# Second mixer of a two-block transformer: the heads' sums of squares from a rounded square and its rest

## The reference, cut to what matters

```
def rmsnorm(x, g):
    x32 = x.astype(jnp.float32)
    y = x32 * lax.rsqrt(jnp.mean(x32 * x32, axis=-1, keepdims=True) + EPS)
    return (y * g.astype(jnp.float32)).astype(x.dtype)
...
    _, o = lax.scan(step, state0, (qc, kc, vc, bc))
    o = o.transpose(1, 0, 3, 2, 4).reshape(bsz, seq, HGRN_HEADS, HGRN_HEAD_DIM)
...
    o = rmsnorm(o, g_norm_w) * jax.nn.silu(g)
    return jnp.einsum('bsd,de->bse', o.reshape(bsz, seq, D_MODEL).astype(h.dtype), w_out)
```

## Time and profile before

| what | us |
| --- | --- |
| median of 3 runs (2376.27 to 2377.44) | 2377.02 |
| the profiled execution's own time | 2377.56 |
| its span in the trace | 2375.8 |
| TensorE busy | 2364.9 |
| VectorE busy | 1326.7 |
| ScalarE busy | 1031.4 |
| GpSimd busy | 62.4 |

### The profile page before, as it was taken

How to read it: one execution, slowest core, us unless ns; L and a number is a source line. 1 busy time by engine, 2 the same in 40 slices (tenths; PEclk the granted TensorE clock), 3 DMA queues, 4 the chain that set the end, 5 groups by cost and what they waited for, 6 DMA issues and landing times.

```text
span 2375.8 us, 30572 instructions
## 1 busy us (share of the span) xinstructions
PE 2364.9 (100%) x11344; PEld 1946.5 (82%) x11344; DVE 1326.7 (56%) x1950; ACT 1031.4 (43%) x1655; POOL 62.4 (3%) x100
## 2 busy tenths in 40 slices
PE   9999999999999999999999999999999999999999
PEld 7777888888888888888888778888888878888887
DVE  6765744432637867444325776777533556677731
ACT  5555522222447855222324664444322545444420
POOL 1000000000002310000000000000001000000000
PEclk9999999999999999999999999999999999999999
DMA  4112222332221113323322113232323222222332
GB/s 159 54 63 80 89 89 90 105 122 91 81 98 63 54 54 98 97 88 101 116 94 89 63 45 116 89 103 92 107 97 107 80 71 96 92 96 95 104 98 83
DMA packets 69332, 214.30 MB, mean 90 GB/s; under 512 B 7280, under 2 KB 18544, under 8 KB 69232
## 3 DMA queue, kind: packets, MB, share of 16 engines
q1 hardware_dynamic: 67696, 210.72, 26.8%
q0 software_dynamic: 1536, 2.21, 0.3%
HBM read 210.80 MB, written 2.10 MB: 90 GB/s over the span
## 4 chain that ended last, share of the span: by engine, by line
PE 95%; DVE 3%; ACT 2%; issue 0%; DMA 0%; SPq 0%; DVEq 0%; ACTq 0%
PE bank L264 26%; PE bank L266 26%; PE bank L265 26%; PE bank L387 5%; PE bank L379 4%; PE bank L1134 1%; PE bank L1521 1%; PE bank L1125 1%; PE bank L1171 1%; PE bank L2061 0%; DVE w_lo L238 0%; DMA raw<-in_w_fox_v 0%; PE bank L2509 0%; PE bank L2497 0%; DVE h L612 0%
## 5 line engine op out<-in xcount | busy, mean ns | idle before, releaser
L264 PE MATMUL bank<-x_hi,w_hi 128*128 128x512 f32 x1792 | 706.9, 394 | 0.1
L266 PE MATMUL bank<-x_hi,w_lo 128*128 128x512 f32 x1792 | 698.5, 390 | 0.0
L265 PE MATMUL bank<-x_lo,w_hi 128*128 128x512 f32 x1792 | 698.3, 390 | 0.0
L238 DVE TENSOR_TENSOR w_lo<-raw,w_hi 128x1024 fp32r<-128x1024 f32 (+1 forms) x367 | 470.4, 1291 | 239.8 <-ACT w_hi L233 239.0
L233 ACT ACTIVATE w_hi<-raw 128x1024 fp32r<-128x1024 f32 (+1 forms) x367 | 403.7, 1109 | 170.7 <-PE bank L266 102.7
L264 PEld LDWEIGHTS bank<-x_hi,w_hi 128*128 128x128 f32 x1792 | 336.7, 188 | 74.1 <-issue 4.2
L266 PEld LDWEIGHTS bank<-x_hi,w_lo 128*128 128x128 f32 x1792 | 336.8, 188 | 70.9
L265 PEld LDWEIGHTS bank<-x_lo,w_hi 128*128 128x128 f32 x1792 | 336.8, 188 | 70.3 <-issue 1.9
L920 DVE TENSOR_TENSOR bank<-bank,rstd 128x512 f32<-128x512 f32 x176 | 122.6, 699 | 292.9 <-PE bank L266 291.8
L264 PE MATMUL bank<-up_a_hi,w_hi 128*128 128x512 f32 (+1 forms) x748 | 282.0, 377 | 0.0
L266 PE MATMUL bank<-up_a_hi,w_lo 128*128 128x512 f32 (+1 forms) x748 | 281.6, 377 | 0.0
(11 more groups left out here) (361 smaller groups left out, 2714.8 us busy)
## 6 DMA issues: line engine op xcount, KB each, us to landing
raw<-in_w_up SPq DMA_DIRECT2D x176, 512.0 KB, 3.3
raw<-in_w_down SPq DMA_DIRECT2D x64, 704.0 KB, 4.4
raw<-in_w_fox_qk SPq DMA_DIRECT2D x16, 512.0 KB, 3.3
raw<-in_w_hgrn_qf SPq DMA_DIRECT2D x16, 512.0 KB, 3.3
raw<-in_w_fox_out SPq DMA_DIRECT2D x8, 512.0 KB, 3.2
raw<-in_w_hgrn_v SPq DMA_DIRECT2D x8, 512.0 KB, 3.4
raw<-in_w_hgrn_g SPq DMA_DIRECT2D x8, 512.0 KB, 3.2
raw<-in_w_hgrn_out SPq DMA_DIRECT2D x8, 512.0 KB, 3.3
```

The lines of the kernel that those rows point to most:

```text
L238: nc.vector.tensor_tensor(w_lo[:, slot, 0:size], raw[:, slot % 2, 0:size], w_hi[:, slot, 0:size].bitcast(F32), ALU.subtract).then_inc(sem( ...
L264: nc.tensor.matmul(out, w[0], x[0], start=first, stop=False)
L265: nc.tensor.matmul(out, w[0], x[1], start=False, stop=False)
L266: return nc.tensor.matmul(out, w[1], x[0], start=False, stop=last)
```

## The change

The sum of squares is made of two parts, in fp32r. ScalarE squares the output twice: once in full into ho, as before, and once rounded into o_hi. GpSimd subtracts o_hi from ho into o_lo. TensorE multiplies a rounded copy of the ones (ones_r, made once by VectorE) by o_hi and then by o_lo, into the same bank. On TensorE the first product waits for the squares, the second for GpSimd's rest (semaphore hg_split). GpSimd makes the rest of head m - 2 between level 2 and level 3 of head m, and those of the last two heads after its loop.

```diff
+        o_hi = hg.take("o_hi", [P, T], F32R)
+        o_lo = hg.take("o_lo", [P, T], F32R)
+        ones_r = hg.take("ones_r", [P, P], F32R)
...
             def norm(o):
 
+                wait(pe, "hg_kdh", o + 1)
+                wait(pe, "hg_ones", 1)
                 wait(pe, "hg_sq", o + 1)
-                wait(pe, "hg_kdh", o + 1)
-                nc.tensor.matmul(ps[4][:], ones[:], ho, start=True, stop=True).then_inc(sem("hg_ms"), 1)
+                nc.tensor.matmul(ps[4][:], ones_r[:], o_hi[:], start=True, stop=False)
+                wait(pe, "hg_split", o + 1)
+                nc.tensor.matmul(ps[4][:], ones_r[:], o_lo[:], start=False, stop=True).then_inc(sem("hg_ms"), 1)
...
-                        nc.scalar.activation(ho, ps[7][:], ACT.Square).then_inc(sem("hg_sq"), 1)
+                        nc.scalar.activation(ho, ps[7][:], ACT.Square)
+                        nc.scalar.activation(o_hi[:], ps[7][:], ACT.Square).then_inc(sem("hg_sq"), 1)
...
             dve_enter(dve, 2)
+            nc.vector.tensor_copy(ones_r[:], ones[:]).then_inc(sem("hg_ones"), 1)
...
+            def split_squares(o):
+                wait(pool, "hg_sq", o + 1)
+                nc.gpsimd.tensor_tensor(o_lo[:], ho, o_hi[:].bitcast(F32), ALU.subtract).then_inc(sem("hg_split"), 1)
             for m in range(HEADS):
                 wait(pool, "hg_b", m + 1)
                 for l in range(1, LEVELS):
+                    if l == LEVELS - 1 and m >= 2:
+                        split_squares(m - 2)
                     wait(pool, "hg_lv", 5 * (m - 1) + l + 1)
...
+            for o in (HEADS - 2, HEADS - 1):
+                split_squares(o)
```

## The result

The changed kernel takes 2387.97 us (median of 6 runs, 2386.95 to 2388.98), the kernel before 2377.71 us in the same comparison. The ratio is 1.0044, 95% interval 1.0034 to 1.0054: 10.3 us slower.

A forecast was written before the change was run, and what follows sets the result against it. TensorE, busy for all of the span, was taken to bound the kernel, with the other engines' round setting the pace after the change. 8.5 + 0.2 + 1.7 = 10.4 us over 2377.0 gave 2387.4, taken as 2387.5; range 2384 to 2391.

The forecast's parts named there:

- The round as the pace: In the steps, the round of VectorE, ScalarE and GpSimd takes 20.1 us, TensorE alone 18.7, so TensorE waits at turn.
- The round's length: Between GpSimd's first instructions of successive heads (the marks): 20.1 us against 18.98; the mark at 847.50 comes 5.9 us later.
- VectorE's last product of the group: In the round from 809.33, taking turns with GpSimd's rest and level 3 makes it end at 815.07, 1.23 us late.
- The clamp and what follows: On VectorE, the clamp comes at 824.56 and the next round's start 4.86 us later, at 829.42.
- The rest's length: GpSimd's subtraction of 128x512 takes 0.99 us, judged from near_q; 1.28 us is the upper bound.
- The wait at turn: TensorE waits some 1.4 us for ScalarE's logarithm at turn, from the second of the rounds on.
- norm(5): In the tail, its rest is made late in the later round: norm ends 8.5 us later, 2.6 even with old rounds.
- Norms 6 and 7: In the tail they wait for square, square and rest: 0.2 us later, with nothing saved in these two.
- The clock: After a wait of over 3 us at norm(5), part of the time runs at 1.2 GHz: 1.7 us lost once.
- The first rival: Rounds keep their length and only norm(5) waits: 4.5 us slower, 2381.5 us; chance 0.20.
- The second: Rival: the round follows TensorE and falls from 18.98 to 18.7 us; not measurably slower, 1.6 us, 2378.6; chance 0.12.
- The third: Rival: the clock falls at every turn, its 1.7 us not hidden, four times: 6.8 us more, 2394; chance 0.05.

The follow-up runs named there:

- e1_no_rest: Changed kernel without GpSimd's rest; the second product takes the rounded square again, so the sum differs: 2376.07 us, ratio 0.9994 to the kernel before.
- e2_rest_unread: Changed kernel with GpSimd subtracting o_hi from itself for heads 0 to 5, TensorE not waiting for it: 2380.38 us, ratio 1.0013 to the kernel before.
- e5_rest_twice: Changed kernel with GpSimd making each rest twice, first into a tile nobody reads: 2398.78 us, ratio 1.0093 to the kernel before.
- e6_head5_ahead: Changed kernel with head 5's rest alone moved ahead of GpSimd's wait for hg_b of head 7: 2384.29 us, ratio 1.0029 to the kernel before.
- e3_rest_ahead: Changed kernel with every rest made ahead of GpSimd's wait for hg_b, not between levels 2 and 3: 2383.93 us, ratio 1.0028 to the kernel before.
- e8_square_alone: Changed kernel with the full fp32 product back and no rest; the second square is made but unread: 2377.58 us, ratio 1.0001 to the kernel before.
- e10_rounded_only: Changed kernel with one rounded square, one product and no rest, so the sum is incomplete: 2374.68 us, ratio 0.9991 to the kernel before.
- e9_pool_then_fp32: Changed kernel with GpSimd's rest for heads 0 to 4 only; heads 5 to 7 keep full fp32 product and one square: 2380.75 us, ratio 1.0016.

## Why the prediction was right

The forecast was 2387.5 us (10.5 over the median of 2377.0), the measurement 2387.97 (10.3 over its comparison's 2377.7). The total is right partly because two errors cancel.

- **The round as the pace.** Right, though the prediction looked for waits of over 1 us at five turns, and there are four, three of them of 0.8 us. The marks are more than 18.98 us apart, TensorE waits at turn, and the runs show that GpSimd's subtraction does it, waited for by TensorE or not: 18.5 to 18.75 us without one (e1_no_rest), 19.38 with one of 1.22 us (e2_rest_unread), 19.65 with 1.48 (beside VectorE), 20.7 with two (e5_rest_twice). No run moves near_q alone, so how much of it is the rest's own collision and how much near_q's is read from rows and not tested.
- **The round's length.** 20.1 was forecast, 19.65 measured; head 7's mark came 3.8 us late and not 5.9. Three terms were mis-sized. VectorE's last product of the group ended 1.10 us late and not 1.23: 817.31 - 811.70 = 5.61 against 4.51 before. The sum took 0.57 + 0.34 = 0.91 us for a product beside half a level, where its own rows had 0.82 and 0.76, and that outweighed a rest taken too short. And from there to near_k VectorE took 822.52 - 817.31 = 5.21 us, not 4.44 + 0.99 = 5.43. The clamp and what follows made up the rest: 831.35 - 822.52 = 8.83, not 8.93.
- **The rest's length.** 0.99 was taken, 1.28 was the bound; alone it lasts 1.26 us, in the row at 853.32 above. The upper bound was right. near_q has one full tensor and one number for eight elements, the rest has two full tensors. With one tensor read twice the rest takes 1.04 us alone, as long as near_q (the row at 852.41 of e2_rest_unread). So the step that failed here is that near_q can stand for an instruction with two full tensors.
- **The wait at turn.** 1.4 us was forecast for each step; it is 1.55 in the first and 0.8 in the others, in line with 19.65 - 18.7 = 0.95. In the first step the wait moved to the norm itself, 2.49 us for the rest, where I had kept it at turn.
- **norm(5).** 8.5 us was forecast from the norm's end of 848.59 to the new one. near started at 848.59 and starts 855.13 in the chain, 6.5 us later, or 6.8 from marks that lay 0.3 us earlier. 3.8 of it is the rounds and 3.0 the norm's own place (2.6 forecast). e6_head5_ahead takes some 2.7 us away by the place.
- **Norms 6 and 7.** 0.2 us was forecast, some 1.3 measured: waits of 0.70 and 0.79 us for a rest of 1.27 us, and a last product that takes 0.50 us from its start when nothing runs ahead of it and not 0.23. In the chains norm(6) ends 8.73 us later than before and norm(7) 9.51, of which 6.54 + 1.71 = 8.25 are norm(5) and the clock. So some 0.5 of the 1.3 is norm(6), for which the prediction worked out nothing, and 0.8 norm(7). This is the term that I sized worst.
- **The clock.** 1.7 us forecast, 1.7 measured in the stretches above. Not every execution has both of the profiled one's falls: four of the six have its mean granted clock, 0.998, the two others 0.999 (2386.95 and 2387.58 us). That the full 1.7 us is in the profiled one is partly luck.

Together 6.8 + 1.3 + 1.7 - 0.3 = 9.5 us, for 9.6 in the span. The mis-sized 5.9 and 0.2 have opposite signs, and that the total came within 0.5 us of the forecast is luck to that extent.

The first rival (rounds unchanged) falls with the marks. The second (not slower) would have needed rounds that shrink; they do in e1_no_rest, where no rest is made. The third (clock down at every turn) falls with a clock of 1.00 over the steps from 764 to 840 of the profiled execution.

In e3_rest_ahead queries lasts 1.10 us beside GpSimd instead of 0.68, and in e2_rest_unread the lo part 2.06 instead of 1.21. The rule of the Trainium skill (SBUF — State Buffer, Who interferes with whom), that a VectorE instruction with two SBUF inputs and a GpSimd instruction reading SBUF exclude each other whole, is borne out by these rows. The rest measured 1.26 us alone. The estimate from the cycles an element that the Trainium skill states (GPSIMD Engine Reference, 3.1 Elementwise), 1.11 us for 512 elements, was nearer than my 0.99 and still short of it.

## What to carry to other kernels

When one engine is busy all of the time, ask of each wait beside it how much room the round of the others has: here it was 1.2 us, and a rest of 1.26 us on GpSimd, the least busy of the four compute engines, used it up, together with near_q, which it pushed beside VectorE's products. GpSimd's time is not free while VectorE works on two tensors in SBUF; moving the instruction moved most of the collision to its neighbours (rounds of 19.45 us instead of 19.65). And look at the last iterations by themselves: a norm with nothing ahead of it had its new operand queued behind work of the next round, and that cost nearly twice what the five regular rounds did, the fall of the clock behind it included.

## What was not expected of the hardware

- **The clock falls in some executions of a kernel and not in others.** In the profiled executions the mean granted clock is 1.000 where no stretch fell, 0.999 with one fall and 0.998 with two, each of 1.7 us of TensorE's time. Read by this mark, 14 of 30, 9 of 24 and 7 of 21 executions of the kernel before had one, and in the median they took 0.7, 0.9 and 0.9 us more than the others. So a single trace does not tell which wait brings a fall. At the first turn, the trace of e8_square_alone has a wait of 1.93 us and a granted clock of 0.83 over 754 to 764; that of e10_rounded_only has a wait of 2.54 us there and stays at 1.00:
```profile
754.00:764.00 10.00, 8.07 (x36) 6.37 (x36) 8.91 (x15) 8.36 (x21) 4.00 (x6) 0.83 0.16 53
```
```profile
754.00:764.00 10.00, 7.46 (x43) 6.31 (x42) 8.88 (x15) 8.40 (x21) 4.03 (x6) 1.00 0.15 53
```
But 9 of 11 executions of e8_square_alone have 1.000, and 7 of 11 of e10_rounded_only have 0.999: over all of them it is the longer wait that goes with more falls. Waits of 0.60 and 0.79 us at norm(5) were followed by a fall in the trace of e6_head5_ahead. Where VectorE, ScalarE and GpSimd set the pace, a fall can cost nothing that is seen: in e9_pool_then_fp32 the five executions with 0.999 have a median of 2380.57 us, the six with 1.000 one of 2380.82. But the second round of e3_rest_ahead, with a fall in it, is 1.2 us longer than its neighbours. What decides whether it comes stays open.
- **The same subtraction is cheaper with one tensor.** On GpSimd, 128x512: alone, 1.26 us with two different tensors and 1.04 with one tensor read twice; beside VectorE, 1.48 and 1.22.
